# A two-layer hybrid decoder trunk on one core: C's two maps in places of their own, A's rotations and two runs of top-eight moved later, and the next layer's first unit of weights split ahead

## The chip, the cores and the metric

One core of a Trainium2 chip runs the whole program. The metric is the device time of one execution in microseconds, the median over runs. TensorE (PE) multiplies matrices into PSUM, VectorE (DVE), ScalarE (ACT) and GpSimd (POOL) do the element work, and SyncE (SP) issues the loads. Each engine takes its own instructions strictly in order and waits on semaphores that others raise.

## The reference, cut to what matters

```python
h = layer_norm(x, ln0_g, ln0_b)                       # x [512, 1024]
for l in range(2):
    pr = split_projection(h @ w_in[l])                # q, k, v of five branches, gates z and g
    o_a = dsa_attention(aq, ak, av, iq, ik, pr['i_w'])# each query keeps 128 keys by an index score
    o_b = moba_attention(bq, bk, bv)
    o_c = rms_norm(diff_attention(cq, ck, cv, lam), diff_norm) * (1 - lam_init)
    o_d = mla_attention(qn, qr, kn, kr, dv)
    o_e = memory_attention(eq, mk, mv)                # 256 memory rows
    y = stack(o_a .. o_e) * silu(z)
    u = einsum('btnc,ncd->btnd', y, w_branch)
    out = sum(sigmoid(g) * u, axis=branch) @ w_out
    h = layer_norm(alpha * h + out, ln_g, ln_b)

# diff_attention: p = softmax(q k^T) for two halves of each head,
#                 (p[0] - lam * p[1]) @ v
```

There are 512 tokens (four tiles of 128) and four heads, so each attention has 16 units of one head and one query tile. All is float32.

## The kernel before

Every product is computed from three matmuls in fp32r: a head (the rounded operand) and a rest (what the rounding left) of both sides, `product3` in L729 to L731. The weights come in units. ORDER (L81) lists the chunks: IX, E, A1, A0, B1, B0, gE0, gE1, gB0, gB1, C0, C1, gA0, gA1, D0, D1, DU, gC0 to gD1, O0, O1. A chunk has four units. For each unit SP loads the raw weights into one of three slots; ACT copies them to fp32r (the head, in step "split"); POOL subtracts head from raw in pieces of 320 columns (the rest, L713); TensorE waits for the rest before the unit's first product. A split stands in the plan behind the last product of the unit three earlier. In the g chunks (gates) a unit has four groups of six matmuls and a fifth group, the branch product u. ACT turns the gate product into tanh, DVE multiplies it with the branch product (L1519), and POOL adds the result to the merged sum (L698, two halves).

The order of all else is one list, PLAN, made by plan(). It lists the product groups (chunk, unit, group), called places here, and hangs other steps behind them. The table PLACES says for each run of steps in which places it begins and ends; spread() distributes the steps evenly by the width of the products. Every engine walks the same list and takes its own part of each step, so what stands behind a place's product stands in that order on all engines. A step that waits holds all that follows on its engine.

The steps: ("qt", b, e) transposes queries and keys of branch b on TensorE; "ev" is ACT's copies of them to fp32r operands, "er" DVE's rests of these (for C four copies and two rests a step, one step for each head and map). ("S", b, u) is the score product into the one PSUM bank S, DVE's masking with the negated maximum (L1398), and ACT's exp (L1104). S of the next unit may start only when the mask of the last one has read the bank (claim("S")). ("T", b, u) transposes the probabilities, ACT copies them, ("V", b, u) multiplies them with the values. "fo" and "fin" divide and gate a head's output; for C, fin has three DVE instructions. C has two maps per unit: S.C.2i and S.C.2i+1, 32 scores in all, and ("W", i) on DVE joins the two (L1450 to L1453) before T.C.i. The index scores ("I") go through ACT's relu and a DVE sum; "top" and "take" are MAX8 and MATCH_REPLACE8 on DVE, 16 rounds for each query tile. The rotary embedding is rotate() on DVE, four instructions; before, A0's and B0's stand directly behind their last products. "kz" zeroes two rests with memsets. diff_steps() gives C's list: three sublists (first, second, third) per unit.

Tally counts the increments of a semaphore and gives the value to wait for from (layer, key).

## Time and profile before

| | us |
|---|---|
| median of 3 timed runs (lowest, highest) | 1393.51 (1391.75, 1394.14) |
| the profiled execution | 1390.51 |
| its span | 1388.9 |
| TensorE busy | 1325.7 (95%) |
| POOL, DVE, ACT busy | 674.3, 655.3, 651.6 |
| TensorE waits for DVE's masks (L1398), all | 16.0 in 20 waits |

The span is the time from the first to the last instruction; the profiled execution has 1.6 us more around it. The mean granted clock of TensorE is 0.992 of full speed. An engine's busy time counts overlapping matmuls once, and the end of a matmul is modelled. The rows below say in brackets how long an engine stood idle before an instruction and what released it.

### The profile page before, as it was taken

To read this page: it belongs to the slowest core of one execution; us is meant where nothing else is said; L and a number is where in the kernel's file an instruction comes from. 1 tells how busy PE (TensorE), PEld (TensorE's weight loads), DVE (VectorE), ACT (ScalarE), POOL (GpSimd) and SP (SyncE) were. 2 spreads that over 40 slices of the span, in tenths; PEclk is the share of its full clock that TensorE was granted. 3 is DMA by queue.
4 is the path that set the end of the run, shared out by engine and by line. 5 is a ranking of instruction groups with operands and counts; after the bars stand their busy time and mean duration, and the time that the engine had idled before them with its cause. 6 is when DMAs were issued, how large, how long until landed. Compare 5 with 4: busy or idle time off the path is not lost.

```text
span 1388.9 us, 19055 instructions
## 1 busy us (share of the span) xinstructions
PE 1325.7 (95%) x6872; PEld 1126.4 (81%) x6872; DVE 655.3 (47%) x1641; ACT 651.6 (47%) x1296; POOL 674.3 (49%) x850
## 2 busy tenths in 40 slices
PE   6999999999999999999999989999999999999995
PEld 5977788888877898888888778888888779888884
DVE  4567746433146553213365774763322675432044
ACT  4455345454276464433245533554524764553232
POOL 3543353354565354467374325424446533645764
PEclk9999999999999999999999999999999999999998
DMA  7322242221331143242322113322124212323221
GB/s 263 109 74 62 70 114 68 65 74 62 103 95 38 39 119 106 58 121 76 119 76 86 61 61 88 95 76 74 57 64 116 61 45 80 96 58 106 84 76 60
DMA packets 147052, 116.47 MB, mean 84 GB/s; under 512 B 5520, under 2 KB 131856, under 8 KB 146704
## 3 DMA queue, kind: packets, MB, share of 16 engines
q1 hardware_dynamic: 146816, 114.22, 27.6%
q8 instruction: 55, 0.90, 0.3%
q10 hardware_dynamic: 144, 1.05, 0.2%
q14 instruction: 37, 0.30, 0.1%
HBM read 112.10 MB, written 3.15 MB: 83 GB/s over the span
## 4 chain that ended last, share of the span: by engine, by line
PE 81%; DVE 10%; ACT 4%; issue 2%; POOL 1%; DMA 1%; SPq 0%; POOLq 0%; DVEq 0%; ACTq 0%
PE product L729 20%; PE product L730 19%; PE product L731 19%; PE context L969 4%; PE scores L941 3%; PE branch_product L729 3%; PE branch_product L731 3%; PE branch_product L730 3%; PE transposed L954 3%; DVE probabilities L1398 1%; DVE index_scores L1364 1%; ACT score_operands L993 1%; DMA residual<-in_x_dram 1%; DVE index_scores L1375 1%; POOL residual L671 1%
## 5 line engine op out<-in xcount | busy, mean ns | idle before, releaser
L713 POOL TENSOR_TENSOR weights_rest<-raw_weights,weights_head 128x320 fp32r<-128x320 f32 (+3 forms) x672 | 544.3, 843 | 387.1 <-ACT weights_head L993 387.1
L729 PE MATMUL product<-weights_head,stationary_head 128*128 128x512 f32 (+3 forms) x768 | 291.2, 379 | 5.9 <-POOL weights_rest L713 5.8
L993 ACT ACTIVATE weights_head<-raw_weights 128x1280 fp32r<-128x1280 f32 (+4 forms) x178 | 198.1, 1114 | 206.6 <-PE product L731 160.9
L730 PE MATMUL product<-weights_rest,stationary_head 128*128 128x512 f32 (+3 forms) x768 | 286.0, 372 | 0.0
L731 PE MATMUL product<-weights_head,stationary_rest 128*128 128x512 f32 (+3 forms) x768 | 285.8, 372 | 0.0
L729 PE MATMUL product<-stationary_head,weights_head 128*128 128x512 f32 x640 | 260.6, 407 | 0.0
L730 PE MATMUL product<-stationary_rest,weights_head 128*128 128x512 f32 x640 | 250.4, 391 | 0.0
L731 PE MATMUL product<-stationary_head,weights_rest 128*128 128x512 f32 x640 | 250.4, 391 | 0.0
L698 POOL TENSOR_TENSOR merged<-merged,activated 128x256 f32<-128x256 f32 x128 | 93.2, 750 | 276.0 <-DVE activated L1519 275.9
L729 PEld LDWEIGHTS product<-weights_head,stationary_head 128*128 128x128 f32 x768 | 145.5, 189 | 27.6 <-POOL weights_rest L713 6.6
L1104 ACT ACTIVATE probabilities<-probabilities,negated_maxima 128x256 f32<-128x256 f32 (+3 forms) x160 | 86.3, 539 | 172.9 <-DVE negated_maxima L1398 172.2
L731 PEld LDWEIGHTS product<-weights_head,stationary_rest 128*128 128x128 f32 x768 | 145.5, 189 | 23.7
L730 PEld LDWEIGHTS product<-weights_rest,stationary_head 128*128 128x128 f32 x768 | 145.7, 190 | 20.5
L731 PEld LDWEIGHTS product<-stationary_head,weights_rest 128*128 128x128 f32 x640 | 120.2, 188 | 26.8
L729 PEld LDWEIGHTS product<-stationary_head,weights_head 128*128 128x128 f32 x640 | 120.6, 188 | 20.1
L730 PEld LDWEIGHTS product<-stationary_rest,weights_head 128*128 128x128 f32 x640 | 120.8, 189 | 19.5
L1519 DVE SCALAR_TENSOR_TENSOR activated<-activated,branch_product 128x512 f32<-128x512 f32 x64 | 44.0, 688 | 157.0 <-PE branch_product L731 156.7
L1165 ACT ACTIVATE activated<-product 128x512 f32<-128x512 f32 x80 | 47.7, 596 | 122.8 <-PE product L731 122.0
L1398 DVE CUSTOM_DVE_ANT_0 probabilities<-scores,consts_sb 128x256 f32<-128x256 f32 (+3 forms) x136 | 60.1, 442 | 87.2 <-PE scores L941 87.0
L969 PEld LDWEIGHTS context<-values_and_gates,probabilities_T 128*128 128x128 f32 x640 | 90.1, 190 | 9.0 <-issue 0.5
L941 PE MATMUL scores<-score_operands 128*128 128x256 f32 (+7 forms) x288 | 78.4, 327 | 17.8 <-DVE negated_maxima L1398 16.0
L993 ACT ACTIVATE probabilities_T<-transposed 128x256 f32<-128x256 f32 (+3 forms) x160 | 67.3, 421 | 48.3 <-PE transposed L954 47.2
(201 smaller groups left out, 1809.0 us busy)
## 6 DMA issues: line engine op xcount, KB each, us to landing
raw_weights<-in_w_in_dram SPq DMA_DIRECT2D x104, 512.0 KB, 3.7
raw_weights<-in_w_in_dram SPq DMA_DIRECT2D x72, 256.0 KB, 2.9
raw_weights<-in_w_branch_dram SPq DMA_DIRECT2D x80, 128.0 KB, 3.7
raw_weights<-in_w_out_dram SPq DMA_DIRECT2D x16, 512.0 KB, 3.6
merged<-in_w_mem_kv_dram SPq DMA_DIRECT2D x8, 512.0 KB, 7.3
raw_weights<-in_w_in_dram SPq DMA_DIRECT2D x8, 416.0 KB, 3.1
raw_weights<-in_w_in_dram SPq DMA_DIRECT2D x8, 296.0 KB, 3.9
residual<-in_x_dram SPq DMA_DIRECT2D x4, 512.0 KB, 10.7
```

The source lines that it names most:

```text
L698: ins = nc.gpsimd.tensor_tensor(m[:, part], m[:, part], TH[:, s, part], ALU.add)
L713: ins = nc.gpsimd.tensor_tensor(WL[:, sw, part], RAW[:, sr, part], WH[:, sw, part].bitcast(F32), ALU.subtract)
L729: nc.tensor.matmul(dst, sh, mh, start=start, stop=False)
L730: nc.tensor.matmul(dst, sh, ml, start=False, stop=False)
L731: return nc.tensor.matmul(dst, sl, mh, start=False, stop=stop)
L941: last = nc.tensor.matmul(S[:, 0:w], lhs, rhs, start=i == 0, stop=i == len(passes) - 1)
L969: last = nc.tensor.matmul(O[:, 0:BW][:, t * HD:(t + 1) * HD], PT[:, i * P:(i + 1) * P], v, start=i == 0, stop=i == w // P - 1)
L993: return nc.scalar.activation(dst, src, ACT.Copy, scale=scale)
L1104: nc.scalar.activation(p, p, ACT.Exp, bias=NMX[:, m:m + 1], scale=-1.0, accum_out=RS[:, j % 2, 2 * t + u % 2 if b == "C" else t:(2 * t + u ...
L1165: nc.scalar.activation(TH[:, s, :], G[u % 2][:], ACT.Tanh, scale=0.5).then_inc(act_out.sem, act_out.step((c, u)))
L1398: nc.vector.tensor_tensor_reduce(probs(b, u)[:, 0:w], S[:, 0:w], bias, -SCALE[b], -TAKEN, ALU.add, ALU.min, NMX[:, u % 4:u % 4 + 1]).then_ ...
L1519: nc.vector.scalar_tensor_tensor(out=TH[:, s, :], in0=TH[:, s, :], scalar=1.0, in1=U[:], op0=ALU.add, op1=ALU.mult).then_inc(used.sem, not ...
```

## The change

C: diff_steps() gives two sublists per unit instead of three, and C's table entry ends one place later; 43 sublists then lie on 55 places, so no place has two. W's two small multiplications become one instruction. A: its rotations leave the place behind A0's products and become a run "A rotations" through B0. The zeroing of the rests moves from A0 to B1, E's queries begin one place later and E's attention two, the top-eight run of tile 1 goes from A1/A0 to A0/B1 and that of tile 2 from A0/B1 to B1/B0. The first unit of the second layer, (IX, 0), is split in a new step "ahead" behind the place (O1, 2, 1) of the first layer; Tally counts by (layer, key) for this, and wait_split finds its value.

```diff
@@ -143,7 +143,7 @@
         if j < NH and m < 2 and i < UNITS:
             third.append(("ev", "C", j, m))
             late = [("er", "C", j, m)]
-        out += [first, second, third]
+        out += [first, second + third]
     return out
@@ -151,14 +151,15 @@
-    ("E attention", ("A1", 1, 2), ("B1", 1, 0), 0.0),
+    ("E attention", ("A1", 2, 0), ("B1", 1, 2), 0.0),
-    ("top of tile 1", ("A1", 1, 1), ("A0", 2, 1), 0.0),
+    ("top of tile 1", ("A0", 0, 2), ("B1", 0, 3), 0.0),
+    ("A rotations", ("B0", 0, 0), ("B0", 2, 3), 0.0),
...
@@ -166,7 +167,7 @@
-    ("C attention", ("gA0", 0, 0), ("D0", 3, 1), 0.0),
+    ("C attention", ("gA0", 0, 0), ("D0", 3, 2), 0.0),
@@ -244,10 +245,10 @@
     steps_of = {
         "index transposes": tiles("ixj"), "index scores": idx, "top of tile 1": tops[1],
         "top of tile 2": tops[2], "top of tile 3": tops[3] + [[("KB",)]], "zero halves": [[("kz",)]],
-        "E queries": [[("qt", "E", 0)], [("ev", "E", 0), ("ev", "E", 1)], [("er", "E", 0), ("er", "E", 1)], [("qt", "E", 1)], [("ev", "E", 2), ("ev", "E", 3)], [("er", "E", 2), ("er", "E", 3)]],
+        "E queries": [[("qt", "E", 0)], [("ev", "E", 0), ("ev", "E", 1)], [("er", "E", 0)], [("er", "E", 1)], [("qt", "E", 1)], [("ev", "E", 2), ("ev", "E", 3)], [("er", "E", 2)], [("er", "E", 3)]],
         "E attention": att_steps("E"), "A attention": att_steps("A"), "B attention": att_steps("B"),
         "C attention": diff_steps(), "D attention": att_steps("D"),
-        "D norms": tiles("rms"), "D latents": tiles("cj"),
+        "A rotations": tiles("rot"), "D norms": tiles("rms"), "D latents": tiles("cj"),
         "roots and C norms": [[("R",)]] + [[("F", j)] for j in range(NH)],
         "norm gains": [[("prm",)]], "lambda": [[("lam",)]],
     }
@@ -259,6 +260,7 @@
         extra[at[("gD1", 3, i)]] += [("mj", 2 * i), ("mj", 2 * i + 1)]
     extra[at[("O0", 0, 0)]] += [("mj", 6), ("mj", 7)]
+    extra[at[("O1", 2, 1)]] += [("ahead",) + WEIGHTS[0]]
     extra[at[("O1", 3, 1)]] += [("l1", 0)]
     extra[at[("O1", 3, 2)]] += [("l1", 1), ("l2", 0)]
     extra[at[("O1", 3, 3)]] += [("l1", 2), ("l2", 1), ("l1", 3), ("l2", 2), ("l2", 3)]
@@ -325,24 +327,21 @@
     def __init__(self, sem, known):
-        self.sem, self.n, self.base, self.known = sem, 0, 0, known
+        self.sem, self.n, self.now, self.known = sem, 0, 0, known
+
+    def place(self, layer, key):
+        return key if key[0] == "first" else (layer,) + key
     def step(self, key, by=1):
         self.n += by
-        self.known.setdefault(key, self.n - self.base if key[0] != "first" else self.n)
+        self.known.setdefault(self.place(self.now, key), self.n)
         return by
     def layer(self, layer):
-        if layer == 1:
-            self.known.setdefault("per_layer", self.n - self.base)
-        if layer == 0:
-            self.known["ahead"] = self.n
-        self.base = self.n
+        self.now = layer
     def at(self, layer, key):
-        if key[0] == "first":
-            return self.known.get(key, 1)
-        return self.known.get("ahead", 0) + layer * self.known.get("per_layer", 0) + self.known.get(key, 1)
+        return self.known.get(self.place(layer, key), 1)
 def build(nc, known, x, mem, ln0_g, ln0_b, w_in, mla_q_norm, w_uq, mla_kv_norm, w_ukv, diff_lam,
@@ -493,6 +492,13 @@
         def w_slot(L, item):
             return (L * len(WEIGHTS) + WEIGHTS.index(item)) % NW
+
+        def wait_split(engine, L, item):
+
+            if L > 0 and item == WEIGHTS[0]:
+                engine.wait_ge(lo_done.sem, lo_done.at(L - 1, ("ahead",) + item))
+            else:
+                engine.wait_ge(lo_done.sem, lo_done.at(L, item))
         def unread(engine, L, item):
@@ -599,7 +605,7 @@
                     elif old[0] == "prm":
                         sp.wait_ge(prm_copied.sem, prm_copied.at(Lo, ("prm",)))
                     else:
-                        sp.wait_ge(lo_done.sem, lo_done.at(Lo, old))
+                        wait_split(sp, Lo, old)
                     if item == ("gD1", 0):
                         sp.wait_ge(t_done.sem, t_done.at(L, ("yj", "C", 1)))
@@ -704,15 +710,17 @@
                         z = VZ[:, 0, t, BW:2 * BW].rearrange("p (h c) -> p h c", h=NH)
                         nc.gpsimd.tensor_tensor(z, z, DN.unsqueeze(1).to_broadcast([P, NH, HD]),
                                                 ALU.mult).then_inc(normed.sem, normed.step(("zn", t)))
-                    if step[0] == "split":
-                        item = step[1:]
+                    if step[0] in ("split", "ahead"):
+                        item, L2 = step[1:], L + (step[0] == "ahead")
+                        if L2 == DEPTH or L > 0 and step == ("split",) + WEIGHTS[0]:
+                            continue
                         pool.wait_ge(head.sem, head.at(L, step))
-                        sw, sr, n = w_slot(L, item), raw_slot(item), size(item[0])
+                        sw, sr, n = w_slot(L2, item), raw_slot(item), size(item[0])
                         for at in range(0, n, PIECE):
                             part = slice(at, min(at + PIECE, n))
                             ins = nc.gpsimd.tensor_tensor(WL[:, sw, part], RAW[:, sr, part], WH[:, sw, part].bitcast(F32),
                                                           ALU.subtract)
-                        ins.then_inc(lo_done.sem, lo_done.step(item))
+                        ins.then_inc(lo_done.sem, lo_done.step(item if L2 == L else step))
         @block.tensor
@@ -748,7 +756,7 @@
                         _, c, u, t = step
                         w, sw = WIDTH[c], w_slot(L, (c, u))
                         if t == 0:
-                            pe.wait_ge(lo_done.sem, lo_done.at(L, (c, u)))
+                            wait_split(pe, L, (c, u))
                         if c == "DU":
                             (na, a), (nb, b) = (("S", S), ("O", O)) if t % 2 == 0 else (("U", U), ("TP", TP))
                             claim(nb)
@@ -1012,13 +1020,15 @@
                 new_layer([head, act_out, copied, exped, moved, rooted, scaled, squared, a_chain], L)
                 for step in PLAN:
                     kind = step[0]
-                    if kind == "split":
-                        item = step[1:]
+                    if kind in ("split", "ahead"):
+                        item, L2 = step[1:], L + (kind == "ahead")
+                        if L2 == DEPTH or L > 0 and step == ("split",) + WEIGHTS[0]:
+                            continue
                         rw = raw[raw_slot(item)]
-                        act.wait_ge(rw.sem, rw.at(L, item))
-                        unread(act, L, item)
+                        act.wait_ge(rw.sem, rw.at(L2, item))
+                        unread(act, L2, item)
                         n = size(item[0])
-                        copy(WH[:, w_slot(L, item), 0:n], RAW[:, raw_slot(item), 0:n]).then_inc(head.sem, head.step(step))
+                        copy(WH[:, w_slot(L2, item), 0:n], RAW[:, raw_slot(item), 0:n]).then_inc(head.sem, head.step(step))
                     elif kind == "ln0" and L == 0 and step[1] < NT:
                         t = step[1]
                         act.wait_ge(summed0.sem, summed0.at(0, ("first", t)))
@@ -1254,6 +1264,10 @@
                             nc.vector.tensor_tensor(X[:, NT - 1, :], X[:, NT - 1, :], LN_IN[:, D:2 * D],
                                                     ALU.add).then_inc(gained0.sem, note(gained0, ("first", "last")))
                             dve.wait_ge(first_in.sem, first_in.at(0, ("first", "c")))
+                    elif kind == "rot":
+                        t = step[1]
+                        dve.wait_ge(copied.sem, copied.at(L, ("A0", t)))
+                        rotate(ST0[:, t, :].rearrange("p (h c) -> p h c", h=8), 8, 8, t, R64, ("A0", t))
                     elif kind == "rms":
                         t = step[1]
                         dve.wait_ge(squared.sem, squared.at(L, ("D0", t)))
@@ -1448,9 +1462,9 @@
                         f = [CF[:, 2 * (i % 2) + m:2 * (i % 2) + m + 1] for m in range(2)]
                         dve.wait_ge(exped.sem, exped.at(L, ("C", 2 * i + 1)))
                         chain(nc.vector.reciprocal(f[1], rs[1]))
-                        chain(nc.vector.tensor_tensor(f[0], f[1], rs[0], ALU.mult))
-                        chain(nc.vector.tensor_tensor(f[1], f[0], LAM[:, 4:5], ALU.mult))
-                        nc.vector.scalar_tensor_tensor(out=first, in0=second, scalar=f[1], in1=first, op0=ALU.mult,
+                        chain(nc.vector.scalar_tensor_tensor(out=f[0], in0=f[1], scalar=LAM[:, 4:5], in1=rs[0], op0=ALU.mult,
+                                                             op1=ALU.mult))
+                        nc.vector.scalar_tensor_tensor(out=first, in0=second, scalar=f[0], in1=first, op0=ALU.mult,
                                                        op1=ALU.add).then_inc(joined.sem, note(joined, step))
                     elif kind == "R":
                         dve.wait_ge(rooted.sem, rooted.at(L, ("D0",)))
@@ -1474,7 +1488,7 @@
                             nc.vector.tensor_copy(KC[:, t, :, HD:HD + MR],
                                                   ST0[:, t, 384:416].unsqueeze(1).to_broadcast([P, NH, MR])).then_inc(v_chain.sem, v_chain.step(("n",)))
                             rotate(ST0[:, t, 0:384].rearrange("p (h c) -> p h c", h=NH)[:, :, HD:HD + MR], NH, MR // 2, t, RM, ("dq", t))
-                        elif c in ("A0", "B0"):
+                        elif c == "B0":
                             dve.wait_ge(copied.sem, copied.at(L, (c, t)))
                             rotate(staged(c[0])[:, t, :].rearrange("p (h c) -> p h c", h=8), 8, 8, t, R64, (c, t))
                         elif c == "C0":
```

On DVE, before, from the gate product of the place (gA0, 1, 4) on (L1519 the gate product, L1398 a mask and its maximum, L1450 to L1453 the step W):

```order
L1398 ISA index_scores,negated_maxima<-scores,consts_sb 128x256
L1398 ISA negated_maxima 128x1
L1519 SCALAR_TENSOR_TENSOR activated<-activated,branch_product 128x512
L1398 ISA probabilities,negated_maxima<-scores,consts_sb 128x384
L1398 ISA negated_maxima 128x1
L1450 RECIPROCAL map_factors<-row_sums 128x1
L1451 TENSOR_TENSOR map_factors<-map_factors,row_sums 128x1
L1452 TENSOR_TENSOR map_factors<-map_factors,lambdas 128x1
L1453 SCALAR_TENSOR_TENSOR index_scores<-index_scores,map_factors 128x256
L1398 ISA probabilities,negated_maxima<-scores,consts_sb 128x384
L1398 ISA negated_maxima 128x1
```

The same place after (L1533 the gate product, L1412 masks, L1464 to L1467 W):

```order
L1533 SCALAR_TENSOR_TENSOR activated<-activated,branch_product 128x512
L1464 RECIPROCAL map_factors<-row_sums 128x1
L1465 SCALAR_TENSOR_TENSOR map_factors<-map_factors,lambdas,row_sums 128x1
L1467 SCALAR_TENSOR_TENSOR probabilities<-probabilities,map_factors 128x128
L1412 ISA index_scores,negated_maxima<-scores,consts_sb 128x256
L1412 ISA negated_maxima 128x1
L1412 ISA probabilities,negated_maxima<-scores,consts_sb 128x384
L1412 ISA negated_maxima 128x1
```

Before, the mask of S.C.4 (384 columns) stood between gate product and W, and S.C.5's behind W. Now W of the unit before follows the gate product, and behind it the mask of S.C.3 (256 columns), then that of S.C.4.

On DVE, after, the place (gA0, 2, 4) and what follows (L1348 and L1350 the rests of C's operands):

```order
L1533 SCALAR_TENSOR_TENSOR activated<-activated,branch_product 128x512
L1464 RECIPROCAL map_factors<-row_sums 128x1
L1465 SCALAR_TENSOR_TENSOR map_factors<-map_factors,lambdas,row_sums 128x1
L1467 SCALAR_TENSOR_TENSOR probabilities<-probabilities,map_factors 128x384
L1412 ISA index_scores,negated_maxima<-scores,consts_sb 128x512
L1412 ISA negated_maxima 128x1
L1348 TENSOR_TENSOR score_operands<-product,score_operands 32x512
L1350 TENSOR_TENSOR score_operands<-product,score_operands 32x512
L1412 ISA probabilities,negated_maxima<-scores,consts_sb 128x128
L1412 ISA negated_maxima 128x1
```

Before, from the same gate product:

```order
L1398 ISA index_scores,negated_maxima<-scores,consts_sb 128x512
L1398 ISA negated_maxima 128x1
L1334 TENSOR_TENSOR score_operands<-product,score_operands 32x512
L1336 TENSOR_TENSOR score_operands<-product,score_operands 32x512
L1519 SCALAR_TENSOR_TENSOR activated<-activated,branch_product 128x512
L1398 ISA probabilities,negated_maxima<-scores,consts_sb 128x128
L1398 ISA negated_maxima 128x1
```

The mask of S.C.7 and the two rests of head 1 now stand behind the gate product and W, directly ahead of the mask of S.C.8, the first score of head 1; before, the rests stood ahead of that gate product.

On DVE, before, around A0's first rotation (L1202 to L1208, with the memsets, and L1398 a mask of E's):

```order
L1381 MAX top_eight<-index_scores 128x8
L1202 TENSOR_TENSOR vector_scratch<-staged_features,consts_sb 128x8x8
L1204 TENSOR_TENSOR vector_scratch<-staged_features,consts_sb 128x8x8
L1206 TENSOR_TENSOR vector_scratch<-staged_features,consts_sb 128x128
L1208 TENSOR_TENSOR staged_features<-vector_scratch 128x8x16
L1325 MEMSET key_rests 64x512 x2
L1398 ISA probabilities,negated_maxima<-scores,consts_sb 128x256
```

After, the first rotation of A, in B0 (L1212 to L1218, with the top-eight run of tile 2 around it):

```order
L1389 MATCH_REPLACE index_scores<-top_eight,index_scores 128x384
L1395 MAX top_eight<-index_scores 128x8
L1212 TENSOR_TENSOR vector_scratch<-staged_features,consts_sb 128x8x8
L1214 TENSOR_TENSOR vector_scratch<-staged_features,consts_sb 128x8x8
L1216 TENSOR_TENSOR vector_scratch<-staged_features,consts_sb 128x128
L1218 TENSOR_TENSOR staged_features<-vector_scratch 128x8x16
L1389 MATCH_REPLACE index_scores<-top_eight,index_scores 128x384
```

No mask of E's follows a rotation any more.

## Rows read from the trace of the kernel before

**Rows 1.** The page, busy time of the engines: us, share of the span, instructions.

```profile
PE 1325.7 (95%) x6872; PEld 1126.4 (81%) x6872; DVE 655.3 (47%) x1641; ACT 651.6 (47%) x1296; POOL 674.3 (49%) x850
```

**Rows 2.** Windows over C's attention, both layers: stretch, length, busy of PE PEld DVE ACT POOL, clock, DMA.

```profile
391.11:481.00 89.89, 82.34 (x428) 69.35 (x427) 60.00 (x168) 59.03 (x129) 43.69 (x54) 1.00 0.19 53
1069.70:1159.60 89.90, 82.34 (x428) 69.31 (x427) 59.99 (x168) 59.04 (x129) 43.67 (x54) 1.00 0.19 54
```

**Rows 3.** Timeline of PE: start, us, instruction, in brackets the wait; A1 to B1.

```profile
77.36 0.66 PE L899 MATMUL transposed<-consts_sb,values_and_gates 128*128 128x128 f32 x4 [0.81 <-ACT values_and_gates L993]
...
92.06 0.45 PE L916 MATMUL branch_product<-score_operands,branch_out_T_rest 96*128 96x384 f32 x1 [1.54 <-ACT activated L1098]
...
142.39 0.51 PE L941 MATMUL scores<-score_operands 128*128 128x256 f32 x2 [2.19 <-DVE negated_maxima L1398]
...
828.31 0.66 PE L969 MATMUL context<-memory_values,probabilities_T 128*128 128x64 f32 x4 [2.82 <-ACT probabilities_T L993]
```

**Rows 4.** Timeline at the join of the layers, PE and ACT.

```profile
711.77 0.41 PE L729 MATMUL product<-weights_head,stationary_head 128*128 128x296 f32 x1 [2.27 <-POOL weights_rest L713]
...
709.35 1.30 ACT L993 ACTIVATE weights_head<-raw_weights 128x592 fp32r<-128x592 f32 x2
```

**Rows 5.** Timeline of PE in C's attention, first layer.

```profile
401.71 0.28 PE L941 MATMUL scores<-score_operands 96*128 96x256 f32 x1
...
401.83 0.40 PE L729 MATMUL product<-stationary_head,weights_head 128*128 128x512 f32 x1
...
406.09 0.27 PE L954 MATMUL transposed<-consts_sb,probabilities 128*128 128x128 f32 x1
...
407.57 0.45 PE L941 MATMUL scores<-score_operands 96*128 96x384 f32 x1 [1.04 <-DVE negated_maxima L1398]
...
407.86 0.39 PE L729 MATMUL product<-stationary_head,weights_head 128*128 128x512 f32 x1
...
410.37 0.39 PE L731 MATMUL product<-stationary_head,weights_rest 128*128 128x512 f32 x1
```

**Rows 6.** Windows of 2 us behind the waits in A0: PEclk is the last but two.

```profile
142.00:144.00 2.00, 1.61 (x7) 1.40 (x8) 1.83 (x8) 1.36 (x4) 0.00 (x0) 0.92 0.65 241
144.00:146.00 2.00, 2.00 (x9) 1.84 (x8) 1.86 (x10) 0.43 (x2) 0.00 (x0) 0.50 0.00 0
146.00:148.00 2.00, 2.00 (x9) 1.58 (x8) 1.68 (x6) 1.02 (x5) 0.00 (x0) 0.73 0.00 0
...
818.00:820.00 2.00, 2.00 (x12) 1.76 (x13) 1.81 (x6) 1.31 (x4) 0.00 (x0) 1.00 0.46 176
```

**Rows 7.** Timeline of DVE in C's attention.

```profile
403.86 0.42 DVE L1398 CUSTOM_DVE_ANT_0 index_scores<-scores,consts_sb 128x256 f32<-128x256 f32 x1
...
406.36 0.69 DVE L1519 SCALAR_TENSOR_TENSOR activated<-activated,branch_product 128x512 f32<-128x512 f32 x1 [2.06 <-PE branch_product L731]
...
409.60 0.69 DVE L1334 TENSOR_TENSOR score_operands<-product,score_operands 32x512 fp32r<-32x512 f32 x1
...
413.42 0.68 DVE L1398 CUSTOM_DVE_ANT_0 index_scores<-scores,consts_sb 128x512 f32<-128x512 f32 x1
...
459.18 0.69 DVE L1519 SCALAR_TENSOR_TENSOR activated<-activated,branch_product 128x512 f32<-128x512 f32 x1 [1.21 <-PE branch_product L731]
...
459.98 0.73 DVE L1451 TENSOR_TENSOR map_factors<-map_factors,row_sums 128x1 f32<-128x1 f32 x1
...
460.74 0.67 DVE L1452 TENSOR_TENSOR map_factors<-map_factors,lambdas 128x1 f32<-128x1 f32 x1
```

**Rows 8.** Timeline of POOL there: the merge behind a gate product.

```profile
459.95 1.44 POOL L698 TENSOR_TENSOR merged<-merged,activated 128x256 f32<-128x256 f32 x2 [7.65 <-DVE activated L1519]
```

**Rows 9.** Timeline of ACT there: an exp, the four operand copies, the tanh.

```profile
409.38 0.61 ACT L1104 ACTIVATE probabilities<-probabilities,negated_maxima 128x384 f32<-128x384 f32 x1
...
410.70 2.42 ACT L993 ACTIVATE score_operands<-product 32x512 fp32r<-32x512 f32 x4
...
414.87 0.58 ACT L1165 ACTIVATE activated<-product 128x512 f32<-128x512 f32 x1
```

8 rows, old and new, of the table PLACES are left out of this document.

## The prediction

> **What bounds the kernel now.** I read the page first: TensorE is busy for 1325.7 of 1388.9 us [rows 1], and no other engine reaches half of the span. All matmuls stay as they are, so the change can only move the 63 us in which TensorE stands, and the time that its clock is halved. The waits of TensorE, each with its place, came next. The start and the end of the program are not touched. What can change lies in three stretches, each once per layer, 678.6 us apart. In C's attention, from 391.11 on, TensorE is busy for 82.34 of 89.89 us: 7.55 us of waits, and the same in the second layer [rows 2]. The second stretch is A1 to B1 (waits at 77.36, 92.06, 142.39 and 828.31, [rows 3]), the third the join of the layers (2.27 us at 711.77, [rows 4]). Then I followed DVE, ACT and POOL through these stretches, since TensorE waits for them, never for a transfer.
>
> Two rules of order are needed below. Each engine takes the plan's steps in one order, and what belongs to a place stands behind that place's products. A place of a g chunk is six products, 0.228 us from start to start (eleven steps from 407.86 to 410.37, [rows 5]), so 1.37 us. The fifth place of each unit is the branch product, and behind it DVE has the gate product (L1519) before anything else.
>
> **E's queries, A's rotations, the two top-eight runs.** Before, E's transposes wait 0.81 us for the copy of E's last tile [rows 3]; one place (1.37 us) later they don't. Both layers: -1.6. The index product at 92.06 waits 1.54 us for a relu that stands on ACT behind the exp of E's first score; E's attention now begins two places later, and relu comes before any exp: 2 x 1.54 = -3.1. At 142.39 S.13 waits 2.19 us for the mask of S.12. On DVE a rotation of A and two memsets stand ahead of that mask; both go from there: -4.4. The 2.82 us at 828.31 come from a rotation ahead of S.14's mask: -2.8. After 142.39 the granted clock is 0.92, 0.50 and 0.73 in three windows of 2 us, half speed (1.2 of 2.4 GHz) for part of them: (0.08 + 0.50 + 0.27) x 2 = 1.7 us lost [rows 6]. After 828.31 the matmuls slow in the same way, and I take the same. That is -3.4. Together -15.3.
>
> What comes in: the four rotations lie in B0, where TensorE waits for nothing of DVE, and B's operands need them long after. Top of tile 1 gets 32 steps in 18 places instead of 22, beside E's masks and the index sums. No row shows that load. The nearest is the wait of 1.54 us of 92.06, where a relu came late behind such steps; I take somewhat less than one of it over both layers, 1.3 us (0 to 6, which is four of them). Sum outside C: **-14.0** (-15.3 to -8).
>
> **The first unit split ahead.** It adds one ACT copy (0.7) and two POOL pieces among the last products, where both idle, and takes them from behind the join. It brings nothing: the 2.27 us at 711.77 are waited for the second unit, IX.1. Its copy starts at 709.35, behind ACT's copies of the second X tile, and POOL's rest follows the copy [rows 4]. Neither moves. Cost 0 (-0.5 to +0.5).
>
> **C's step W.** One of four DVE instructions goes, 32 times. Its own time is 0.16 us, but 0.67 where POOL works (460.74, [rows 7]). Nothing waits for that alone; it enters the sums below.
>
> **C's places.** Before, both maps of a unit share the fifth place of a unit of weights in six of 16 cases: S.odd waits for the mask of S.even, 0.39 to 1.04 us (1.04 at 407.57, [rows 5]), 4.2 us a layer. These waits go, and so do the others of the 7.55. But in all five fifth places that hold a W, W and the mask of S.odd now stand behind the gate product, with S.even of the next unit due one place later. Before, S.odd had at least two places.
>
> Take the first, S.3 in unit 1 of gA0. t is the start of the first instruction behind the branch product. The gate product starts at t + 0.27 (406.09 on TensorE, 406.36 on DVE, [rows 5, 7]). It lets POOL start its two merges of 0.72 [rows 8]. W's small product starts 0.80 behind the gate product (459.18 to 459.98: its 0.61 and the reciprocal's 0.19) and runs until the first merge ends (460.74, 0.76 later), so W's last instruction starts at t + 1.83. It waits out the second merge, 0.67, and takes 0.3 (128 columns) to 0.55 (384) itself. W ends at t + 2.8 to 3.05; the mask of S.3 adds 0.43 (403.86, [rows 7]). S.4 can start at t + 3.25; TensorE is there at t + 0.12 + 1.37 + 0.04 = t + 1.53. Wait: **1.7** (0.5 if POOL is never met).
>
> S.7 and S.8 are worse. S.8 also needs C's next operands, whose two rests (0.69 and a gap each, 409.60, [rows 7]) now stand behind the mask of S.7 in the same place, directly ahead of S.8's. W to t + 3.05, mask of 512 columns 0.69 (413.42), rests 0.12 + 1.43: S.8 at t + 5.35 against t + 0.24 + 1.37 + 0.39 + 0.25 = t + 2.25. Wait 3.1. On ACT, moreover, the operand copies (2.42 us at 410.70) stand behind S.5's exp, ahead of the tanh (414.87, [rows 9]) that the gate product needs. Taken from S.3 on (mask t + 3.2, exp of 256 columns 0.7, copies 2.4, copy and exp of unit 2 1.0, exp of 384 columns 0.8 as at 409.38, copies 2.4, tanh 0.6) the tanh ends at t + 11.1, TensorE's branch product at t + 9.6: about 1.2 more. Wait: **4.3** (1.9 with neither POOL nor tanh late).
>
> The others by the same steps: S.12 0.85, S.15 0.8 (behind fin of head 0), S.16 3.9 (as S.8), S.20 0.85, S.23 1.8 (rests and fin of head 1, 2.8 to 3.5 us, stand two places ahead of it), S.31 0.45. Sum 14.65 a layer against 7.55: +7.1, twice **+14.2**. A wait also costs some 0.17 in the matmuls behind it (0.29 from the score at 407.57 to the next product, 0.12 from the one at 401.71, [rows 5]); 12 waits a layer become 8: **-1.4**.
>
> The clock: it fell after a wait of 2.19 and after one of 2.82, and did not after 2.19 at 817.96 (1.00 in the window behind it, [rows 6]) or the 2.27 of 711.77. The four waits of S.8 and S.16 are about 4 us, broken by two short instructions. I take three falls of 1.7: **+5.1** (0 to 6.8).
>
> C in all: 14.2 - 1.4 + 5.1 = +17.9. Bounds: with neither POOL nor a late tanh 5.5 us of waits a layer, -4.1 - 1.4 = -5.5; with all four falls and each wait longer by a fifth, +25.
>
> The Trainium skill bears on two of these. "SBUF — State Buffer", section "Who interferes with whom", has VectorE instructions with two SBUF inputs locked out for the whole of a GpSimd instruction that reads SBUF. By that the 0.16 us instruction of W is worth a whole merge, as in the row of 460.74, and the last one of W waits even though its neighbour is gone; without the lock the first wait above would be 0.5 instead of 1.7. "TensorE: Matmul & The Clock Gate", section "HAM oscillation — how this bites in real kernels", warns that idle gaps of TensorE between bursts halve its clock. It speaks against fewer but longer waits, which is what this change makes of C: all four long waits would cost, 6.8 instead of the 5.1 taken, and the time would be 1399.1 (rival 6).
>
> **The sum.** -14.0 + 0 + 17.9 = **+3.9 us**. On the profiled execution (1390.51: the span of 1388.9 and 1.6 around it) that is 1394.4. The median of the timed runs, 1393.51, lies 3.0 above it, and I put the 3.9 on the median: **1397.4**.
>
> **The rivals.**
> 1. *Faster: C's queue is shorter.* If ACT's tanh is in time, S.8 and S.16 wait 3.1 and C's waits are 11.3 a layer: +7.5 - 1.4. With one fall of the clock (1.7) that is +7.8, and with -14 outside -6.2: 1387.3. For it: the tanh at 414.87 held nothing up, with the same work on ACT. Against: the operand copies come two places nearer to it now, and behind a mask that is itself late. It decides when the tanh of gA0's third unit ends before its branch product does. Chance 0.25.
> 2. *Much faster: the maps apart are free*, as the edit means: POOL is met nowhere, -5.5 in C, -19.5: 1374. For it is only that nothing forces POOL's merge to begin at once; against it the rows of 459.98 and 460.74. 0.06.
> 3. *The clock holds* after the new waits: 3.9 - 5.1 = -1.2: 1392.3. 0.18.
> 4. *Slower still: DVE is overfull in A0.* Top of tile 1 is 1.78 steps a place now (32 in 18), beside a mask and an index sum in the same places. If masks then come 0.4 late at a dozen places a layer, some 6 more than taken: 1403. 0.08.
> 5. *The split ahead works on the join*: the 2.27 us go: 3.9 - 2.3 = +1.6: 1395.1. For it: ACT and POOL have less to do there. Against: the order of rows 4. 0.05.
> 6. *Every long wait halves the clock*: +1.7 on the forecast: 1399.1. For it the 1.7 at 142.39 and 828.31, against it 817.96. 0.12, inside the forecast's 0.38.
>
> **How the numbers follow.** The forecast, 1397.4 with an own range of 1392 to 1403, has 0.38 (with rival 6), the rivals 1 to 5 0.25, 0.06, 0.18, 0.08 and 0.05. What a measurement of this kernel can't tell from no change is 0.2%, 2.8 us: 1390.7 to 1396.3. Faster: rivals 1 and 2, 0.31, less 0.01 at the edge: 0.30. Same: rivals 3 and 5, 0.23. Slower: the forecast and rival 4, 0.46, and 0.01 for what is left. The range that leaves out 2 in 10 goes from 1384 (past rival 1, short of 2) to 1405 (past rival 4).
>
> **What the profile after would show.** TensorE's waits at S.13, V.12, the index product and E's transposes gone, and the clock at 1.00 through A0 and B1. In C no S.odd waits, but S.4, S.12 and S.20 wait for a mask, S.8 and S.16 for rests (L1350), the latter the longest of the kernel, with the granted clock at 0.5 behind some of them; C's stretch some 7 us longer. The wait of 2.3 us for the rest of IX.1 still there. I am wrong if C's stretch is no longer than 90 us, if the long waits stay under 2 us, or if new waits of more than 3 us a layer appear between A1 and B0.

## The result, and the profile after

| | before | after |
|---|---|---|
| median of the timed runs (lowest, highest), us | 1392.63 (1388.57, 1394.14) | 1382.05 (1379.84, 1384.15) |
| the profiled execution, us | 1390.51 | 1384.15 |
| its span, us | 1388.9 | 1382.5 |
| mean granted clock of TensorE | 0.992 | 0.985 |

The change makes the kernel faster: ratio 0.9931, 95% interval 0.991 to 0.9951, some 10 us. The forecast was +3.9 with a range down to 1384. The time lies below the range, on the other side of no change.

In the page of the kernel after, TensorE is busy 2.3 us longer than in [rows 1], with the same matmuls, and the span is 6.4 shorter: it waits 8.7 less, and part of it runs slower.

```profile
PE 1328.0 (96%) x6872; PEld 1130.7 (82%) x6872; DVE 661.8 (48%) x1609; ACT 653.3 (47%) x1296; POOL 669.9 (48%) x850
```

To see where, I found the same matmuls of the long runs of products in both traces and subtracted their starts. What one stretch adds to the difference (after minus before, us; the times are those of the trace before):

| stretch | forecast | layer 1 | layer 2 |
|---|---|---|---|
| start, to 60 | 0 | +2.54 | |
| join, 700 to 730 | 0 | | -0.02 |
| A1 to B0 (60 to 205, 730 to 884) | -15.3 + 1.3 in both | -8.38 | -11.39 |
| B's first scores (205 to 250, 884 to 930) | 0 | +1.08 | +1.07 |
| C (390 to 540, 1068 to 1230) | +17.9 in both | +4.79 | +3.97 |
| all others | 0 | 0 | 0 |

The sum is -6.3; the spans differ by 6.4. The start is chance: the transfer of an X tile landed 1.4 us later, and the first products, between TensorE's waits for weights, ran at half clock for longer (0.58 granted from 30 to 40 us, 0.83 before). In the executions of the experiments it is 0.4 us shorter to 2.4 us longer than in the one of before, whatever the kernel. Without it the change is worth -8.9; what is left to the 10.6 of the medians lies inside the scatter of the kernel before, whose timed runs went from 1388.6 to 1397.2 over all comparisons.

**Outside C.** The waits of [rows 3] are all gone, and the granted clock is 1.00 from 120 to 150 and from 790 to 850. Of the products' path these rows of TensorE are left or new (start, duration, instruction; in brackets the idle time ahead of it and what ended it; L949 is S, L977 V, L962 T, L737 a product):

```profile
129.06 0.66 PE L977 MATMUL context<-memory_values,probabilities_T 128*128 128x64 f32 x4 [0.54 <-DVE diff_out L1421]
206.24 0.38 PE L949 MATMUL scores<-score_operands 128*128 128x256 f32 x1 [1.50 <-DVE negated_maxima L1412]
711.78 0.40 PE L737 MATMUL product<-weights_head,stationary_head 128*128 128x296 f32 x1 [2.26 <-POOL weights_rest L721]
```

The wait at 206.24 was 0.44 before, the 2.26 of the join answers to [rows 4] and is as it was.

**C.** TensorE over C's attention and all that follows until both kernels have done the same work (the score product behind 509.80), before and then after. Columns: stretch, its length, busy time (instructions), granted clock, DMA share, GB/s.

```profile
391.11:509.80 118.69, 110.78 (x626) 1.00 0.24 69
1069.70:1188.44 118.74, 110.83 (x626) 1.00 0.24 69
```

```profile
386.34:509.80 123.46, 114.98 (x626) 0.96 0.23 66
1059.39:1182.10 122.71, 114.20 (x625) 0.97 0.23 67
```

Idle time goes from 7.91 and 7.91 to 8.48 and 8.51: +0.6 a layer. Busy time goes up by 4.2 and 3.4. C is longer by the clock, hardly by waits. The waits of the first layer, the longest ones:

```profile
402.68 0.30 PE L962 MATMUL transposed<-consts_sb,probabilities 128*128 128x128 f32 x1 [1.08 <-DVE probabilities L1467]
413.46 0.52 PE L962 MATMUL transposed<-consts_sb,probabilities 128*128 128x128 f32 x3 [1.78 <-DVE probabilities L1467]
415.53 0.44 PE L949 MATMUL scores<-score_operands 96*128 96x128 f32 x1 [1.54 <-DVE score_operands L1350]
438.96 0.52 PE L962 MATMUL transposed<-consts_sb,probabilities 128*128 128x128 f32 x3 [1.05 <-DVE probabilities L1467]
441.00 0.30 PE L949 MATMUL scores<-score_operands 96*128 96x128 f32 x1 [1.52 <-DVE score_operands L1350]
```

And the granted clock behind S.8 (415.53), in windows of TensorE:

```profile
412.00:414.00 2.00, 0.52 (x3) 0.97 0.00 0
414.00:416.00 2.00, 0.47 (x2) 0.50 0.00 0
416.00:418.00 2.00, 2.00 (x5) 0.50 0.17 27
418.00:420.00 2.00, 2.00 (x10) 0.50 0.52 186
420.00:422.00 2.00, 2.00 (x10) 0.82 0.03 8
```

It falls during the second of two waits that follow each other, to half speed (1.2 of 2.4 GHz), and stays there for some 5 us of products. At 441.00, and at the same two places in the second layer, it falls within 1.5 us behind such a pair of waits: four falls in C, none there in the kernel before.

### The profile page after: what moved, and what is told of

It is laid out like the page before. It is cut to its first block, busy times and chain, and to the rows that moved or that the text cites. A ratio compares the mean times of both kernels' runs of the same rounds, so it can differ in the third digit from the quotient of the medians.

```text
span 1382.5 us, 19021 instructions
## 1 busy us (share of the span) xinstructions
PE 1328.0 (96%) x6872; PEld 1130.7 (82%) x6872; DVE 661.8 (48%) x1609; ACT 653.3 (47%) x1296; POOL 669.9 (48%) x850
## 3 DMA queue, kind: packets, MB, share of 16 engines
q10 hardware_dynamic: 144, 1.05, 0.2%
## 4 chain that ended last, share of the span: by engine, by line
PE 79%; DVE 12%; ACT 4%; issue 2%; POOL 1%; DMA 1%; SPq 0%; POOLq 0%; DVEq 0%; ACTq 0%
PE product L737 19%; PE product L738 18%; PE product L739 18%; PE context L977 5%; PE scores L949 3%; PE transposed L962 3%; PE branch_product L737 2%; PE branch_product L739 2%; PE branch_product L738 2%; DVE index_scores L1389 2%; DVE top_eight L1395 1%; DMA residual<-in_x_dram 1%; ACT score_operands L1001 1%; POOL residual L677 1%; DVE vector_scratch L1214 1%
## 5 line engine op out<-in xcount | busy, mean ns | idle before, releaser
L737 PE MATMUL product<-weights_head,stationary_head 128*128 128x512 f32 (+3 forms) x768 | 291.4, 379 | 7.8 <-POOL weights_rest L721 7.6
L737 PE MATMUL product<-stationary_head,weights_head 128*128 128x512 f32 x640 | 263.5, 412 | 0.0
L737 PEld LDWEIGHTS product<-weights_head,stationary_head 128*128 128x128 f32 x768 | 145.7, 190 | 29.8 <-POOL weights_rest L721 8.4
L737 PEld LDWEIGHTS product<-stationary_head,weights_head 128*128 128x128 f32 x640 | 121.8, 190 | 20.8
L1533 DVE SCALAR_TENSOR_TENSOR activated<-activated,branch_product 128x512 f32<-128x512 f32 x64 | 44.0, 687 | 154.5 <-PE branch_product L739 149.6
L1412 DVE CUSTOM_DVE_ANT_0 probabilities<-scores,consts_sb 128x256 f32<-128x256 f32 (+3 forms) x136 | 60.4, 444 | 110.8 <-PE scores L949 110.6
L977 PEld LDWEIGHTS context<-values_and_gates,probabilities_T 128*128 128x128 f32 x640 | 89.8, 190 | 9.9 <-issue 1.4
L949 PE MATMUL scores<-score_operands 128*128 128x256 f32 (+7 forms) x288 | 77.7, 324 | 10.3 <-DVE score_operands L1350 6.1
## 6 DMA issues: line engine op xcount, KB each, us to landing
residual<-in_x_dram SPq DMA_DIRECT2D x4, 512.0 KB, 11.4
```

What stands on the lines that cost most here:

```text
L737: nc.tensor.matmul(dst, sh, mh, start=start, stop=False)
L949: last = nc.tensor.matmul(S[:, 0:w], lhs, rhs, start=i == 0, stop=i == len(passes) - 1)
L977: last = nc.tensor.matmul(O[:, 0:BW][:, t * HD:(t + 1) * HD], PT[:, i * P:(i + 1) * P], v, start=i == 0, stop=i == w // P - 1)
L1412: nc.vector.tensor_tensor_reduce(probs(b, u)[:, 0:w], S[:, 0:w], bias, -SCALE[b], -TAKEN, ALU.add, ALU.min, NMX[:, u % 4:u % 4 + 1]).then_ ...
L1533: nc.vector.scalar_tensor_tensor(out=TH[:, s, :], in0=TH[:, s, :], scalar=1.0, in1=U[:], op0=ALU.add, op1=ALU.mult).then_inc(used.sem, not ...
```

## The experiments

All times are medians; the stretches are read as in the table above.

**e1. C's order undone** (the rest of the change stays).

```diff
-        out += [first, second + third]
+        out += [first, second, third]
...
-    ("C attention", ("gA0", 0, 0), ("D0", 3, 2), 0.0),
+    ("C attention", ("gA0", 0, 0), ("D0", 3, 1), 0.0),
```

> The changed kernel with C's steps given out as before (three lists per unit, so both maps share places again); all else of the change stays. Theory: C's part of the change costs 4.8 us in the first layer and 4.0 in the second, nearly all of it TensorE at half clock behind two long waits, so this comes out 8.7 us below the changed kernel, about 1373.4, with C's stretch at 118.7 us instead of 123.5 and the clock at 1.00 through it. Rival (the prediction's sum): C costs 17.9, so 1364. Second rival (C's part is what gained, and the rest of the change did little): 1390 or more.

Measured: 1372.49 (ratio to before 0.9868, 0.9846 to 0.989), 9.6 below the kernel after. C's stretch is 117.4 us in both layers with the clock at 1.00. C's order costs the change some 11.4 us by the stretches (4.79 + 1.28 and 3.97 + 1.35), the other parts gain; in the medians 1.6 of it are hidden by a fall of the clock at the join, of which more below. The 1.3 below the 118.7 of before is W's merged instruction, alone in the old order.

**e2. C's order alone** (on the kernel before).

```diff
-        out += [first, second, third]
+        out += [first, second + third]
...
-    ("C attention", ("gA0", 0, 0), ("D0", 3, 1), 0.0),
+    ("C attention", ("gA0", 0, 0), ("D0", 3, 2), 0.0),
```

> The kernel before with C's order alone changed (two lists per unit, end one place later), with W still four instructions of DVE. Theory: +8.7 us over the kernel before, about 1401.3, plus up to 1 us, since W's chain is one instruction longer where POOL merges. Rival: if the merged instruction of W carried a large part (0.7 us at each of four long waits), +12 or more. Second rival (C's part gains): below 1392.

Measured: 1411.64 (1.0146, 1.0118 to 1.0175), 20 us slower than before: C takes 10.0 and 10.4 longer, so the first rival is right and my theory gave less than half. T's first three waits in C's first layer, L954 of this kernel (two more follow, 2.25 at 447.40 and 1.06 at 462.05):

```profile
407.84 0.30 PE L954 MATMUL transposed<-consts_sb,probabilities 128*128 128x128 f32 x1 [1.89 <-DVE probabilities L1453]
421.09 0.52 PE L954 MATMUL transposed<-consts_sb,probabilities 128*128 128x128 f32 x3 [2.63 <-DVE probabilities L1453]
436.11 0.30 PE L954 MATMUL transposed<-consts_sb,probabilities 128*128 128x128 f32 x1 [1.06 <-DVE probabilities L1453]
```

With the merged W the first two are 1.08 and 1.78 and the third 0.24: 0.8 us each, for an instruction of 0.16 us alone ([rows 7]: 0.67 where POOL works). The clock has its part in the 10: the granted clock of C is 0.95 here, and of the 5.2 us by which C of the first layer is longer here than in the kernel after, 4.0 are idle time. In the changed order the merged instruction is worth 5.2 and 6.4 us a layer.

**e3. C's operands one unit earlier** (on the kernel after).

```diff
-        if i == 4:
+        if i == 3:
             third.append(("qt", "C", 1))
-        j, m = divmod(i + 3, 4)
+        j, m = divmod(i + 4, 4)
```

> The changed kernel with C's next operands (copies on ACT, rests on DVE) given out one unit earlier, so that the rests no longer stand between the mask of S.7 and S.8 (S.15 and S.16); W and the masks stay where they are. Theory (the clock falls because two waits follow each other): S.8 and S.16 no longer wait, T.2 and T.6 wait about 1 us, the clock stays at 1.00, C's stretch is about 118.5 us and the time about 9 us below the changed kernel, 1373. Rival (the wait for W alone, 1.8 us, is enough to halve the clock): only 1.5 us of idle goes at four places and the clock still falls, 1377 to 1379.

Measured: 1374.77 (0.9879, 0.9853 to 0.9905). C is 119.5 and 117.9 us. S.8 and S.16 no longer wait. But T.0 waits 1.97 in place of 1.08, in both layers: ACT's operand copies (2.42 us from 397.75) now end at the tanh of that place, and the gate product starts 1.18 behind S.3 instead of 0.27. And the clock tells the layers apart. TensorE's two rows, and the window behind each:

```profile
403.28 0.30 PE L962 MATMUL transposed<-consts_sb,probabilities 128*128 128x128 f32 x1 [1.97 <-DVE probabilities L1467]
1073.78 0.30 PE L962 MATMUL transposed<-consts_sb,probabilities 128*128 128x128 f32 x1 [1.97 <-DVE probabilities L1467]
```

```profile
404.00:406.00 2.00, 2.00 (x6) 0.50 0.00 0
1074.00:1076.00 2.00, 2.00 (x10) 1.00 0.05 8
```

One and the same wait halves the clock in the first layer and not in the second, and the stretches differ by 1.6 us. The theory holds for what the rests cost; of the clock it was half right.

**e4. A's rotations alone** (on the kernel before).

```diff
+    ("A rotations", ("B0", 0, 0), ("B0", 2, 3), 0.0),
...
-                        elif c in ("A0", "B0"):
+                        elif c == "B0":
```

> The kernel before with A's four rotations alone moved from A0's places into B0. Theory: the waits of 2.19 us at 142.39 and 817.96 shrink to under 1 (the two memsets stay ahead of that mask) and the 2.82 at 828.31 goes, with the half clock behind them, while B's score in gE0 waits 1.1 longer in both layers: -2.5 in the first layer, -5 in the second, in all 7 to 8 us below the kernel before, 1385. Rival (the memsets and the top-eight steps, not the rotations, hold the masks): under 3 us gained. B's wait in gE0 tells on its own whether the rotations cause it: 1.5 with them in B0, 0.45 without.

Measured: 1381.37 (0.993, 0.9909 to 0.9952). A1 to B0 gains 4.1 and 7.1, more than expected: the waits of 2.19 and 2.82 are gone altogether, so the memsets alone held nothing. B's second score still waits only

```profile
208.34 0.38 PE L942 MATMUL scores<-score_operands 128*128 128x256 f32 x1 [0.45 <-DVE negated_maxima L1403]
```

so the rotations by themselves are not what costs there.

**e7 and e8. E's moves alone, and the top-eight runs' moves alone** (each on the kernel before; the table's entries of the change, no others, and in e7 E's rests as steps of their own, as in the change).

```diff
e7:
+    ("E queries", ("A1", 0, 0), ("A1", 2, 0), 0.0),
+    ("E attention", ("A1", 2, 0), ("B1", 1, 2), 0.0),
...
+    ("E out", ("B1", 2, 0), ("B1", 2, 2), 0.0),
e8:
+    ("zero halves", ("B1", 3, 0), ("B1", 3, 0), 0.0),
...
+    ("top of tile 1", ("A0", 0, 2), ("B1", 0, 3), 0.0),
+    ("top of tile 2", ("B1", 1, 0), ("B0", 3, 0), 0.0),
```

> The kernel before with E's queries, E's attention and E's output alone in their new places. Theory: the waits of 0.81, 1.54, 0.42, 0.39 and 0.59 us (E's transposes, and the index products for their relu) go in both layers, 4.3 us a layer by the stage table of the changed kernel, if the top-eight runs have no part in it; but the masks of E meet A's rotations at other places, so the waits of 2.19 and 2.82 change too: 8.6 below the kernel before if they go, about 0 if they grow by as much. Rival (the prediction's): only 0.81 and 1.54 a layer go, 4.7 in all. The two are told apart by the waits on the relu.

> The kernel before with the top-eight runs of tiles 1 and 2 (and the two memsets) alone in their new places. Theory: B's second score in gE0 waits longer than 0.45 us here, since the rotations alone did not do it; the 2.19 us wait keeps the rotation but loses the memsets and gets top-eight steps of tile 1, so it changes by under 1. In all within 3 of the kernel before. Rival (tops and rotations only together make B's wait): 0.45 stays.

Measured: e7 1384.21 (0.9926, 0.9902 to 0.995), A1 to B0 2.6 and 5.1 shorter. e8 1390.0 (0.997, 0.995 to 0.9989), +0.3 and -2.7; it also lost 1.6 at the join, to the clock, and 1.7 in C of the first layer alone, where two waits for masks are 0.35 and 0.89 longer; why only there stays unexplained. The relu waits (index product for ACT's L1098) tell most. Per layer they are 2.9 us before, 2.4 with E's moves alone, 0.56 with the top-eight runs moved alone, and 0 to 0.15 with both. The longest of e7, and the one of e8:

```profile
97.44 0.45 PE L916 MATMUL branch_product<-score_operands,branch_out_T_rest 96*128 96x384 f32 x1 [1.00 <-ACT activated L1098]
```

```profile
91.65 0.45 PE L916 MATMUL branch_product<-score_operands,branch_out_T_rest 96*128 96x384 f32 x1 [0.56 <-ACT activated L1098]
149.29 1.12 PE L969 MATMUL context<-memory_values,probabilities_T 128*128 128x64 f32 x4 [2.54 <-ACT probabilities_T L993]
```

The theory of e7 falls on the relu (E's transposes no longer wait, as it said): moving E's attention moves these waits, and what removes them is the top-eight run that leaves DVE free beside E's first masks. A likely chain is that relu stands on ACT behind an exp, and the exp behind a mask that is late on DVE; no run shows each link. The relu and E's transposes make 1.3 us a layer of what e7 gains. The rest comes from the waits in A0, with the rotations still there: in the first layer 0.79, 0.88 and 0.32 stand in place of 2.19 and the clock no longer falls, in the second 0.52 and 0.89 stand in place of 2.19 and 2.82. So the parts don't add up: between A1 and B0 the gains of e4, e7 and e8 sum to 6.4 and 14.9 us, and the whole change gains 8.4 and 11.4. Alone, e8 gets a wait of 2.54 elsewhere (rotations still in A0). B's wait in gE0 is 0.44 to 0.46 in e4, e7 and e8: it takes at least two of the parts together to make it 1.50; which two, no run shows.

**e6. Tile 3's top-eight run five places later** (on the kernel after).

```diff
-    ("top of tile 3", ("gE0", 0, 1), ("gE1", 2, 3), 0.0),
+    ("top of tile 3", ("gE0", 1, 1), ("gE1", 2, 3), 0.0),
```

> The changed kernel with the top-eight run of tile 3 begun five places later (second place of gE0's second unit instead of second place of its first). Theory (the new 1.1 us at B's second score come from DVE's backlog of rotations, top-eight steps and B's rests): the wait of 1.50 us at 206.2 and 879.3 shrinks below 0.5 or goes, 2 to 3 us below the changed kernel over both layers, 1379.5. Rival (the gate product and the mask behind it hold S.1, whatever stands ahead): 1.5 stays, 1382.

Measured: 1379.84 (0.9899, 0.9875 to 0.9924). The wait goes from 1.50 to 0.95, not below 0.5. The median fits the theory by luck: by the stretches B's first scores are only 0.33 us a layer shorter; the two profiles differ otherwise by the start (1.9 shorter here) and by the clock in the second layer's C (0.6 longer). That steps standing ahead on DVE make the wait is borne out by e11 (below), where the run starts four places later still and the wait is gone.

**e5. W ahead of the fifth place** (on e3).

```diff
-            second.insert(0, ("W", i - 1))
+            first.append(("W", i - 1))
```

> The kernel of e3 with W moved from ahead of S.odd's mask to behind S.even's, so that no W stands behind a gate product in a fifth place. Theory (the waits for W come from its standing behind the gate product, where POOL's two merges slow it): T.0, T.2, T.4, T.6 and T.8 no longer wait, no clock falls in C, C's stretch goes from some 118.7 us to 112, in all 13 below e3: 1362. Rival (DVE's whole load in C sets the pace, or W now stands in front waiting for the exp of S.odd and delays the next mask): the waits move to S.odd and C keeps 117 or more, 1372 or more.

Measured: 1360.67 (0.9758, 0.9735 to 0.9781), better than both kernels. No T waits in C at all. TensorE in C:

```profile
383.73:496.42 112.69, 109.50 (x625) 1.00 0.27 72
1045.94:1158.69 112.75, 109.54 (x626) 1.00 0.27 73
```

3.2 us of idle time instead of 8.5, and the clock at 1.00. The queue behind the gate product was the cause of T's and S's waits: e3 took the rests out of it and S.8 and S.16 stopped waiting; this run took W out and T stopped too. With both elsewhere C is 6 us a layer shorter than before, 3.8 of it by the order (e10, below) and the rest by the merged instruction. DVE's whole load isn't the limit.

**e9 and e10. The split ahead undone, and W as four instructions** (each on e5; e9's code goes back to one kind of split, e10's to the two small multiplications).

```diff
e9:
-    extra[at[("O1", 2, 1)]] += [("ahead",) + WEIGHTS[0]]
e10:
-                        chain(nc.vector.scalar_tensor_tensor(out=f[0], in0=f[1], scalar=LAM[:, 4:5], in1=rs[0], ...
+                        chain(nc.vector.tensor_tensor(f[0], f[1], rs[0], ALU.mult))
+                        chain(nc.vector.tensor_tensor(f[1], f[0], LAM[:, 4:5], ALU.mult))
```

> The kernel of e5 without the split ahead: the next layer's first unit is split behind the join again. Theory (as in the prediction): the wait of 2.27 us for IX.1 at the join stays and nothing else waits; within 0.5 us of e5, 1360.7, apart from 1.6 more if the clock falls behind that wait, as it did in e1, e3, e7 and e8 and not in the others. Rival (the split ahead carries part of the gain): a wait for IX.0 appears ahead of it, 2 us or more.

> The kernel of e5 with W as four instructions of DVE again. Theory: the merged instruction is worth much only where W stands between a gate product and an operand that TensorE waits for (5.2 and 6.4 us a layer between the kernel with C's order alone and the changed one); with W off those places its 0.2 to 0.7 us meets slack, and this is within 3 us of e5, 1361 to 1364. Rival (the instruction is worth 5 us or more a layer anywhere, since DVE is full in C): 1370 or more.

Measured: e9 1360.73 (0.977, 0.9747 to 0.9793), as e5 in each stretch behind the start to 0.1 us; the split ahead is worth nothing, as forecast. e10 1367.38 (0.9816, 0.9793 to 0.9839), 6.7 above e5 and outside both expectations: C is 2.2 and 2.1 longer than in e5, and 1.6 are a fall of the clock at the join. So the instruction is worth 1.3 a layer in the old order (e1), 2.1 here and 5 to 6 behind the gate product.

**e11. Two waits that were left** (on e5): fin goes one unit later, tile 3's run starts nine places later.

```diff
-            third.append(("fin", "C", (i - 3) // NT))
+            fin = [("fin", "C", (i - 3) // NT)]
...
-        out += [first, second + third]
+        out += [first + held, second + third]
...
-    ("top of tile 3", ("gE0", 0, 1), ("gE1", 2, 3), 0.0),
+    ("top of tile 3", ("gE0", 2, 0), ("gE1", 2, 3), 0.0),
```

(held is the fin of the unit before.)

> The kernel of e5 with fin (the norm sums of a head) one unit later in C, and the top-eight run of tile 3 begun nine places later, with B's second score done. Theory: the wait of 1.28 us at 445.3 (S.23, behind C's rests and fin) shrinks below 0.5 and so does the 1.5 in gE0, about 4 us below e5, 1357. Rival (fin merely delays the mask behind its new place, and B's wait comes from top of tile 2 and the rotations ahead of B's rests): 1360 to 1361.

Measured: 1356.66 (0.9739, 0.9717 to 0.9762), the best version, 25 us below the kernel after. B's wait in gE0 is gone, the wait at S.23 too, and C is

```profile
381.78:493.27 111.49, 109.52 (x626) 1.00 0.27 73
```

**e12. The kernel after once more.**

> The changed kernel once more, unchanged, on the same chip as the three beside it. Theory: its waits and the places where the clock falls in C are the same to 0.1 us in both layers, 1382; only the start (first weights) and single clock falls differ. Rival (the falls of the clock in C are chance from run to run): in one of the four places the granted clock stays at 1.00 and the layer is 1.6 us shorter.

Measured: 1383.54 (0.9924, 0.9899 to 0.995). Every stretch as in the first profile to 0.15 us (C +4.65 and +3.96), with all four falls in C; the start is 1.5 shorter. So the falls in C belong to the kernel, and the start does not.

## Why the prediction was wrong

**The step that failed** is the sum over C's places, "14.65 a layer against 7.55: +7.1, twice +14.2". Measured in brackets, as the 7.55 are, C's waits are

| | predicted | measured, layer 1 |
|---|---|---|
| S.4 | 1.7 | 1.08 (at T.0, ahead of it) |
| S.8 | 4.3 | 1.78 (T.2) + 1.54 |
| S.12, S.20 | 0.85 each | 0.24 each (T.4, T.8) |
| S.15, S.31 | 0.8, 0.45 | none |
| S.16 | 3.9 | 1.05 (T.6) + 1.52 |
| S.23 | 1.8 | 0.45 |
| sum | 14.65 | 7.9 |

The idle time of the stretch grew by 0.6 a layer, so the term is +1.2 and not +14.2 - 1.4. Two errors are in it. (t is, as in the prediction, the start of the first instruction behind the branch product.) *Units*: I worked out delays from start to start and set them against waits in brackets, which begin only where the last matmul is modelled to end; T, which waits first, then takes 0.25 itself. S.4 comes at t + 3.00 (predicted t + 3.25) against t + 1.53 if nothing held it: a delay of 1.47, of which the brackets show 1.08. S.8 comes at t + 6.0, predicted t + 6.55; the delay is 3.8, the brackets 3.3. *The others, taken from these two by analogy*: at S.12 and S.20, TensorE has eight matmuls of context ahead of T, 1.0 us, which cover the same late W; at S.16 the tanh was 0.3 late, not 1.2 (at S.8 0.95), and S.16 comes 5.35 behind S.15; what I added for fin and rests at S.15, S.23 and S.31 hardly met anything.

The queue on DVE was read rightly. But what waits for it first is T, which the prediction does not name, and the waits that the edit brings (7.9 us) hardly outweigh the 7.55 that it takes away: what is left of C's loss is mostly the clock. DVE, behind S.3 and S.7 of the kernel after (L1533 gate product, L1464 to L1467 W, L1412 mask, L1348 and L1350 rests), reads as the prediction has it:

```profile
400.20 0.69 DVE L1533 SCALAR_TENSOR_TENSOR activated<-activated,branch_product 128x512 f32<-128x512 f32 x1 [1.02 <-PE branch_product L739]
401.00 0.72 DVE L1465 SCALAR_TENSOR_TENSOR map_factors<-map_factors,lambdas,row_sums 128x1 f32<-128x1 f32 x1
401.75 0.78 DVE L1467 SCALAR_TENSOR_TENSOR probabilities<-probabilities,map_factors 128x128 f32<-128x128 f32 x1
402.45 0.41 DVE L1412 CUSTOM_DVE_ANT_0 index_scores<-scores,consts_sb 128x256 f32<-128x256 f32 x1
...
410.73 0.69 DVE L1533 SCALAR_TENSOR_TENSOR activated<-activated,branch_product 128x512 f32<-128x512 f32 x1 [1.67 <-ACT activated L1175]
411.52 0.71 DVE L1465 SCALAR_TENSOR_TENSOR map_factors<-map_factors,lambdas,row_sums 128x1 f32<-128x1 f32 x1
412.27 1.05 DVE L1467 SCALAR_TENSOR_TENSOR probabilities<-probabilities,map_factors 128x384 f32<-128x384 f32 x1
413.24 0.68 DVE L1412 CUSTOM_DVE_ANT_0 index_scores<-scores,consts_sb 128x512 f32<-128x512 f32 x1
413.96 0.69 DVE L1348 TENSOR_TENSOR score_operands<-product,score_operands 32x512 fp32r<-32x512 f32 x1
414.68 0.70 DVE L1350 TENSOR_TENSOR score_operands<-product,score_operands 32x512 fp32r<-32x512 f32 x1
```

beside POOL's merges and ACT's late tanh:

```profile
400.97 1.42 POOL L704 TENSOR_TENSOR merged<-merged,activated 128x256 f32<-128x256 f32 x2 [2.36 <-DVE activated L1533]
411.50 1.41 POOL L704 TENSOR_TENSOR merged<-merged,activated 128x256 f32<-128x256 f32 x2 [5.74 <-DVE activated L1533]
```

```profile
410.10 0.60 ACT L1175 ACTIVATE activated<-product 128x512 f32<-128x512 f32 x1
```

One thing in it was too dear: W's last instruction does not wait out the second merge and then take its own 0.3 or 0.55. It takes 0.78 and 1.05 in all, where I had 0.97 and 1.22. Rival 1, "C's queue is shorter", had the right direction, for the wrong reason: the tanh was late, as I held against it. Its number was also added up wrongly: with 3.1 at S.8 and at S.16 the sum of 14.65 becomes 12.65 and not 11.3, so by its own terms it gives some 1390 and not 1387.3.

The other terms, in the order of the prediction:

- *E's transposes and index product, -1.6 and -3.1*: both waits went, and so did three more relu waits of 0.4 to 0.6 us (at 102.59, 109.71 and 121.80 of the trace before) which I had left standing; 1.4 a layer not counted. The reason given, that E's attention begins later, carries only a part; the top-eight run carries the rest of the relu waits (e7, e8).
- *Rotations, -4.4 - 2.8 - 3.4 = -10.6*: e4 has -11.2. Right for the rotations moved alone; E's moves alone also take away part of these waits and one fall of the clock (e7), so in the whole change the two can't be told apart.
- *New between A1 and B0, +1.3*: 0.54 a layer at 129.06, and 1.1 a layer at B's second score in gE0. There I had written that nothing waits for DVE in B0 and B's operands need the rotations long after. The price came one stage later, from DVE's backlog (e6, e11). By stretches: outside C and the start -17.6, against -14.0.
- *Split ahead, 0*: right (e9).
- *W's merged instruction*: I gave it no term of its own. It is worth 2.6 us in the old order and 11.7 in the new one (after against e2); in the forecast it sat inside the chain for S.4 and S.8, where it was counted.
- *Clock in C, +5.1*: three falls taken, four came, and busy time grew by 7.6. Rival 6 was right on the count and low on the price (1.7 a fall, 1.9 measured). The long waits are under 2 us each, which I had named as a sign of being wrong; two of them in a row still made a fall.

In all C cost 8.8 and not 17.9: +1.2 of waits where I had +12.8, +7.6 of clock where I had +5.1. With -17.6 in place of -14.0 outside, that is -8.9, and the sign of the whole.

## What to carry to other kernels

Work out waits in one unit: an idle time in brackets is shorter than the delay of the start behind it, by the modelled tail of the last matmul and the short instruction that waits first (here some 0.4 us), and a sum of one kind can't be set against a sum of the other. Price each late operand at its own place with what the waiting engine still has to do there, not by analogy to the worst one. When an edit puts two steps apart, look at what they now stand behind: here W and the next operands' rests behind the gate product undid what the free places gave, and moving just these two turned the same edit from a loss of 5 to 6 us a layer (the kernel after against e1) into a gain of 4 to 5 (e5 against e1).
